# Attention's values on two column halves of the array, with normalised probabilities as the moving operand

## The reference

```python
s = jnp.einsum('bcqhgd,bcshd->bchgqs', qc, kb) * (A_HEAD_DIM ** -0.5)   # + bias, masked
m = jnp.maximum(jnp.max(s, axis=-1, keepdims=True), sink)
p = jnp.exp(s - m)
denom = jnp.sum(p, axis=-1, keepdims=True) + jnp.exp(sink - m)
o = jnp.einsum('bchgqs,bcshd->bcqhgd', p / denom, vb)
...
mix = jnp.concatenate([y_a, y_b], axis=-1)      # attention | retention
x = x + mix @ w_out
```

## Time and profile before

| | |
|---|---|
| median of 3 runs | 576.05 us (575.78 to 576.2) |
| the profiled execution's own time | 576.34 us |
| its span | 574.2 us |
| PE busy in the span | 549.9 us (96%) |
| DVE busy | 423.5 us (74%) |
| ACT busy | 359.3 us (63%) |
| mean granted TensorE clock | 0.995 |

### The profile page before, as it was taken

One profiled execution on the slowest core, in us unless ns is written; L12 is line 12 of the kernel. 1 busy time (PEld: TensorE's weight loads), 2 busy tenths in 40 slices (PEclk: granted clock), 3 DMA queues, 4 the chain that ended last, 5 costly groups with the idle time before them and its releaser, 6 DMA issues.

```text
span 574.2 us, 8097 instructions
## 1 busy us (share of the span) xinstructions
PE 549.9 (96%) x2782; PEld 451.3 (79%) x2783; DVE 423.5 (74%) x572; ACT 359.3 (63%) x477; POOL 116.7 (20%) x102
## 2 busy tenths in 40 slices
PE   3999999999999999998999999999999999999992
PEld 3988878888878888876788888888888888888860
DVE  2664577454764843377988889888898888988887
ACT  4563554781134363335778887788877888778823
POOL 3350000000000000002443234432244323411100
PEclk9999999999999999999999999999999999999998
DMA  8989212203020236677999999999999999999173
GB/s 299 373 277 387 58 36 74 74 20 128 1 73 1 74 111 226 231 276 272 344 390 373 371 366 365 368 367 335 346 372 389 372 359 374 369 389 339 34 294 146
DMA packets 72044, 144.32 MB, mean 251 GB/s; under 512 B 3794, under 2 KB 13322, under 8 KB 71888
## 3 DMA queue, kind: packets, MB, share of 16 engines
q1 hardware_dynamic: 65936, 124.96, 61.7%
q0 software_dynamic: 6080, 19.00, 9.5%
HBM read 132.77 MB, written 14.69 MB: 257 GB/s over the span
## 4 chain that ended last, share of the span: by engine, by line
PE 85%; DVE 6%; DMA 4%; issue 2%; ACT 1%; SPq 0%; POOL 0%; POOLq 0%; DVEq 0%
PE ps L1317 24%; PE ps L1319 23%; PE ps L1318 23%; PE ps L1324 6%; PE ps L1429 2%; PE ps L1466 2%; PE ps L1454 2%; DMA arena<-y_dram 1%; PE ps L1497 1%; PE ps L1399 1%; DMA arena<-norm_g 1%; PE ps L1420 1%; DVE res L1304 1%; DMA arena<-h_dram,meta 1%; PE ps L1337 1%
## 5 line engine op out<-in xcount | busy, mean ns | idle before, releaser
L1117 DVE TENSOR_TENSOR lo_ring<-arena,hi_ring 128x2048 fp32r<-128x2048 f32 x94 | 215.1, 2291 | 28.5 <-ACT hi_ring L808 27.4
L1317 PE MATMUL ps<-hi_ring,act_hi 128*128 128x512 f32 x576 | 232.6, 404 | 0.5 <-DVE act_lo L911 0.5
L1319 PE MATMUL ps<-hi_ring,act_lo 128*128 128x512 f32 x576 | 225.2, 391 | 0.0
L1318 PE MATMUL ps<-lo_ring,act_hi 128*128 128x512 f32 x576 | 224.7, 390 | 0.0
L808 ACT ACTIVATE hi_ring<-arena 128x2048 fp32r<-128x2048 f32 x94 | 180.2, 1917 | 18.6 <-PE ps L1319 18.6
L1317 PEld LDWEIGHTS ps<-hi_ring,act_hi 128*128 128x128 f32 x576 | 108.3, 188 | 27.4 <-issue 6.0
L1319 PEld LDWEIGHTS ps<-hi_ring,act_lo 128*128 128x128 f32 x576 | 108.1, 188 | 23.6
L1318 PEld LDWEIGHTS ps<-lo_ring,act_hi 128*128 128x128 f32 x576 | 108.4, 188 | 20.2
L901 DVE SCALAR_TENSOR_TENSOR lo_ring<-arena,over,hi_ring 128x512 fp32r<-128x512 f32 x40 | 29.4, 748 | 33.5 <-ACT hi_ring L640 33.5
L911 DVE TENSOR_TENSOR act_lo<-ps,act_hi 128x512 fp32r<-128x512 f32 x64 | 41.7, 683 | 11.6 <-ACT act_hi L669 5.8
L563 POOL DMA_INDIRECT y_dram<-y,row_info x15 | 16.1, 1073 | 149.6 <-issue 149.6
(11 more groups left out here) (197 smaller groups left out, 564.1 us busy)
## 6 DMA issues: line engine op xcount, KB each, us to landing
arena<-w_gate SPq DMA_DIRECT2D x32, 1024.0 KB, 15.2
arena<-w_up SPq DMA_DIRECT2D x32, 1024.0 KB, 15.8
arena<-w_down SPq DMA_DIRECT2D x32, 1024.0 KB, 15.6
arena<-w_in SPq DMA_DIRECT2D x16, 512.0 KB, 7.8
y_dram<-arena POOLq DMA_DIRECT2D x8, 512.0 KB, 11.8
arena<-w_out SPq DMA_DIRECT2D x4, 1024.0 KB, 5.2
arena<-y_dram SPq DMA_DIRECT2D x8, 512.0 KB, 7.1
arena<-w_in SPq DMA_DIRECT2D x3, 1024.0 KB, 12.9
```

Source lines behind the costliest of these rows:

```text
L1117: nc.vector.tensor_tensor(lo(N1 + n12), raw(n12), hi(N1 + n12).bitcast(F32), ALU.subtract).then_inc(lo_done, 1)
L1317: nc.tensor.matmul(dst, a_hi, b_hi, start=start, stop=False)
L1318: nc.tensor.matmul(dst, a_hi, b_lo, start=False, stop=False)
L1319: return nc.tensor.matmul(dst, a_lo, b_hi, start=False, stop=stop)
```

## The change

1. `softmax_denom` goes on: after the reciprocal, DVE multiplies the probabilities in `prob` (4 heads by 128 keys for u < 2, by 192 after that) by it and raises `p_scaled`. `turn_prob` waits for that where it waited for `exp_done`, and for the copies of the unit before.
2. `turn_prob` lays the four heads' transposes side by side, one bank per key block; ACT copies whole banks, into a buffer per key group.
3. `values` runs once per token tile instead of once per unit, in slots 5, 9, 13 and 17. The stationary operand is 64 columns of values, the moving one 512 columns of probabilities (4 heads by 128 queries), key group 0 writes PSUM partitions 0 to 63 and group 1 writes 64 to 127. The result is channels by tokens already; DVE copies it to `mix` (512 columns, four times) where it scaled 256 columns eight times.
4. `turn_mix(0)` goes. `mix_hi(0)` and `mix_lo(0)` read `mix` in SBUF, in slot 28. PE waits for the gate's silu (`silu_done`) in front of each tile of group 11 in its place.
5. The rows of `w_out` that belong to attention arrive in the new order of channels, in two transfers of 64 partitions in place of one of 128 (groups 11 and 13).

```diff
@@ DVE
                 step_done(nc.vector.reciprocal(r_denom, denom))
-
-            def attention_out(u):
-                t, kv = u // 2, u % 2
-                dve.wait_ge(o_ready, u + 1)
...
-                nc.vector.tensor_tensor(mix[:, t, 256 * kv:256 * kv + 256].rearrange("p (h c) -> p h c", h=4),
-                                        ps[:, 6, 0:256].rearrange("p (h c) -> p h c", h=4),
-                                        r_denom.unsqueeze(2).to_broadcast([P, 4, A_DIM]), ALU.mult).then_inc(mix_a, 1)
+                w0 = P if u < 2 else CHUNK
+                nc.vector.tensor_tensor(prob[:, :, w0:], prob[:, :, w0:],
+                                        r_denom.unsqueeze(2).to_broadcast([P, 4, 2 * P - w0]), ALU.mult).then_inc(p_scaled, 1)
+
+            def attention_out(t):
+                dve.wait_ge(o_ready, t + 1)
...
+                nc.vector.tensor_copy(mix[:, t, 0:512], ps[:, 6, :]).then_inc(mix_a, 1)
...
-                if k in VALUE_SLOTS:
-                    attention_out(VALUE_SLOTS.index(k))
+                if k in VALUE_SLOTS[1::2]:
+                    attention_out(VALUE_SLOTS.index(k) // 2)
@@ PE
             def turn_prob(u):
                 if u:
-                    pe.wait_ge(mix_a, u)
-                else:
-                    pe.wait_ge(va_copied, 1)
+                    pe.wait_ge(pt_copied, probs_value(u - 1))
+                if u >= 2:
+                    pe.wait_ge(mix_a, u // 2)
...
-                pe.wait_ge(exp_done, 4 * (u + 1))
...
+                pe.wait_ge(p_scaled, u + 1)
+                for b in range(1 if u < 2 else 0, 2):
+                    ins = turn(6 + b, [prob[:, hh, b * P:(b + 1) * P] for hh in range(4)])
                 ins.then_inc(p_turned, 1)
 
-            def values(u):
...
-                        ins = nc.tensor.matmul(ps[:, 6, hh * A_DIM:(hh + 1) * A_DIM], prob_t[:, hh, b, :],
-                                               va[:, t - 1 + b, kv * A_DIM:(kv + 1) * A_DIM], start=(b == b0), stop=(b == 1))
+            def values(t):
...
+                for b in range(b0, 2):
+                    for kv in range(2):
+                        rows = slice(kv * A_DIM, (kv + 1) * A_DIM)
+                        ins = nc.tensor.matmul(ps[rows, 6, :], va[:, t - 1 + b, rows], prob_t[kv][b],
+                                               start=(b == b0), stop=(b == 1))
                 ins.then_inc(o_ready, 1)
...
+                        pe.wait_ge(silu_done, T + t + 1)
...
-                if k == MIX_A_SLOT:
-                    turn_mix(0)
@@ SP
-                    sp.wait_ge(m_turned, 2 * T)
+                    sp.wait_ge(m_turned, T)
+                    sp.wait_ge(m_lo, T)
...
+                    if half == 0:
+                        for kv in range(2):
+                            sp.dma_start(as_chunks(dst)[kv * A_DIM:(kv + 1) * A_DIM, :, :],
+                                         w_out_heads[:, 4 * kv:4 * kv + 4, 512 * cols:512 * cols + 512]
+                                         ).then_inc(w1_in[slot1(g)], 16)
```

More of the change, by code:

```diff
@@ L94 @@
 SCM_OFF = (0, 512, 896, 1152)
+TWO_PART_OUT = (NA + NB, NA + NB + 2)
 def log_gamma(h):
@@ L118, in w1_value, with probs_value @@
 def w1_value(g):
-    return 16 * sum(2 if NA <= h < NA + NB else 1 for h in range(g % RING1, g + 1, RING1))
+    return 16 * sum(2 if NA <= h < NA + NB or h in TWO_PART_OUT else 1 for h in range(g % RING1, g + 1, RING1))
+def probs_value(u):
+    return u + 1 if u < 2 else 2 * u
 def build(nc, x, norm1_g, w_in, attn_sinks, rel_bias, ret_gn_g, w_out, norm2_g, rg_w, rg_b, re_w, re_b,
@@ L193, in build @@
         bias_pairs = region(O_BIAS, A_HEADS * WIN).rearrange("p (i a j) -> p a i j", i=4, a=2)
-        prob_t = region(O_PT, 1024).rearrange("p (h b q) -> p h b q", h=4, b=2)
+        prob_t = [[region(O_PT, 512), region(O_PT + 512, 512)],
+                  [region(O_MIX + b * D + 512, 512) for b in range(2)]]
         scm = region(O_SCM, 1280)
@@ L248, in build @@
         w_out_v = w_out.rearrange("a (k p) n -> p (a k) n", p=P)
+        w_out_heads = w_out.rearrange("a (k p) n -> p (a k) n", p=A_DIM)
         w_gate_v = w_gate.rearrange("a e (k p) n -> (a e) p k n", p=P)
@@ L700, in copy_prob_t @@
                 act.wait_ge(p_turned, u + 1)
[L701 to L704, removed]
+                for b in range(1 if u < 2 else 0, 2):
+                    nc.scalar.copy(prob_t[u % 2][b], ps[:, 6 + b, :]).then_inc(pt_copied, 1)
             def copy_rot(n):
@@ L711, in mix_hi @@
             def mix_hi(part):
+                if part == 0:
+                    act.wait_ge(mm_done, tile_value(NA + NB - 2, T - 1))
                 for t in range(T):
-                    act.wait_ge(m_turned, T * part + t + 1)
+                    if part:
+                        act.wait_ge(m_turned, t + 1)
+                        rows = ps[:, 4 + t, :]
+                    else:
+                        act.wait_ge(mix_a, t + 1)
+                        rows = mix[:, t, 0:512]
                     nc.scalar.activation(ht_hi[:, 4 * part:4 * part + 4, t * P:(t + 1) * P],
-                                         ps[:, 4 * part + t, :].rearrange("p (k s) -> p k s", k=4),
-                                         ACT.Copy).then_inc(m_hi, 1)
+                                         rows.rearrange("p (k s) -> p k s", k=4), ACT.Copy).then_inc(m_hi, 1)
             def copy_x2(half, t):
@@ L1049, in mix_lo @@
                 for t in range(T):
-                    row_lo(ht_lo[:, 4 * part:4 * part + 4, t * P:(t + 1) * P], 4 * part + t,
-                           ht_hi[:, 4 * part:4 * part + 4, t * P:(t + 1) * P], m_hi, T * part + t + 1, m_lo)
+                    rows = ps[:, 4 + t, :] if part else mix[:, t, 0:512]
+                    dve.wait_ge(m_hi, T * part + t + 1)
+                    nc.vector.tensor_tensor(ht_lo[:, 4 * part:4 * part + 4, t * P:(t + 1) * P],
+                                            rows.rearrange("p (k s) -> p k s", k=4),
+                                            ht_hi[:, 4 * part:4 * part + 4, t * P:(t + 1) * P].bitcast(F32),
+                                            ALU.subtract).then_inc(m_lo, 1)
             def norm2(t):
@@ L1468, in retention_values, with turn_mix @@
                 ins.then_inc(ro_ready, 1)
[L1470 to L1474, removed]
+            def turn_mix():
+                pe.wait_ge(mix_b, B_HEADS)
                 for t in range(T):
[L1476 to L1479, removed]
+                    turn(4 + t, [mix[:, t, 512 + i * P:512 + (i + 1) * P] for i in range(4)]).then_inc(m_turned, 1)
             def turn_x2(n):
@@ L1547, in _ @@
                     turn_v()
-                if k in VALUE_SLOTS:
-                    values(VALUE_SLOTS.index(k))
+                if k in VALUE_SLOTS[1::2]:
+                    values(VALUE_SLOTS.index(k) // 2)
                 if k in TURN_SLOTS:
@@ L1562, in _ @@
                 if k == MIX_B_SLOT:
-                    turn_mix(1)
+                    turn_mix()
                 if (g, t) in TURN_X2_STEPS:
```

25 lines of the change are left out of this document (11 added, 14 removed).

## The result

The changed kernel takes 599.58 us (598.7 to 601.09) against 576.12 us; the recorded ratio is 1.0368 with a 95% interval of 1.033 to 1.0405 (the quotient of these two medians alone is 1.041, just above it). The forecast was 592.0 us in a range of 588 to 597. The sign and the place were right, the size was too small by about a third: + 23.5 us by the medians (+ 21 by the ratio) against + 15.9.

The account below looks back on a forecast made before the run. PE was taken as the bound: + 16.7 (transposes later), + 0.4 (last values), - 1.7 (`turn_mix(0)` gone), + 0.5 (copy wait) = + 15.9 us on 576.34, 592.2; less 0.3 to the median, forecast 592.0, range 588 to 597.

Parts of the forecast that it names:

- What bounds the kernel: Attention and experts: PE is busy nearly throughout (71.97 of 73.00 us, 276.69 of 277.00), so added work or waits lengthen the time.
- The loop: Attention: each unit's transposes now wait for DVE's multiplication, closing a ring; seven turns sum to 79.47 us, last transposes 16.7 later.
- The 0.05 from DVE to PE: Attention: the step from the end of DVE's multiplication to PE's transposes, added to the multiplication's 0.95 us for 1.00.
- What PE saves is not on the path: Attention: PE's 7.8 us of work without values, against a ring of 12.0, leaves it idle; only slot 17's values count.
- the rival of the wait never felt: Attention: DVE's product is ready before PE wants it, so only PE's savings stay, - 5.6 us, 570.5; chance 0.04.
- The values on halves: Attention: four 512-column matmuls, two passes each, run in pairs; 2.1 us at slot 17 against 1.7 before, + 0.4.
- the wait of 0.5 for the last copy of values: Retention, slot 31: its values now stand right behind the tile and need ACT's last copy of the values; + 0.5 us.
- The clock: Rival, attention: the clock falls in PE's new gaps of about 4.2 us, costing 2 to 7 us, 594 to 599; chance 0.18.
- its own sign of being wrong: Changed profile: waits at the transposes below 1 us, clock below full inside the mixers, or PE idle less in the experts.
- The other side: Rival, attention: with 2.7 us of slack on DVE the wait is never felt and the time is 570.5; chance 0.04.
- not idle by choice: Attention: DVE's split at 85.14 waits for ACT's split, exponentials, logits and PE's scores in turn, so DVE has no slack.

Follow-up runs that it names:

- e8_fill_keep: The changed kernel with idle matmuls in front of the eight transposes and eight more in front of the first expert's rows; 591.89 us, ratio 1.0231.
- e2_early: The changed kernel with DVE's denominator, reciprocal and multiplication moved from slot 2u+2 to slot 2u, in front of that slot's split; 573.33 us, ratio 0.9916.
- e3_loop_only: The kernel before with only DVE's multiplication added, PE's transposes waiting for it and the output copied unscaled, no column halves; 602.37 us, ratio 1.0425.
- e1_fill: The changed kernel with 5 to 17 idle identity multiplications on PE in front of each unit's wait for the scaled probabilities; 596.05 us, ratio 1.0323.
- e11_after_split: e2_early with DVE's scaling one instruction later, behind the split of slot 2u instead of in front of it; 580.69 us, ratio 1.0053.

## Why the prediction was wrong

- *What bounds the kernel* was right: PE has no slack, and DVE's place in the queue is read from the timelines, not from busy shares. e8_fill_keep and e2_early show both.
- *The loop*, + 16.7 us of starts shifted: right. Without falls of the clock (e8_fill_keep) every loop lies within 0.05 us of its sum, and the whole distance is + 16.4 against the sum's + 15.9. Even with the falls five of seven loops lie within 0.35 us. e3_loop_only shows the loop as the cause by itself. The 0.05 from DVE to PE had no row of before behind it; it measures 0.05 in e8_fill_keep and up to 0.15 in the changed kernel.
- *What PE saves is not on the path*: right in the changed kernel. e2_early brings the savings out once the loop is short: 3.9 us, less than the 5.6 that the rival of the wait never felt had summed, and with 1.4 us of waits for the multiplication left.
- *The values on halves*: taken as 2.1 us a call, measured 1.87. The pass of 0.46 us was read from a row of 2.32 that contains the last matmul's run through the array; by the starts a pass is 0.43. `turn_mix(0)` and the wait of 0.5 for the last copy of values came about as priced: behind the last transposes e8_fill_keep is 0.6 us shorter than before, against 0.4 - 1.7 + 0.5 = - 0.8.
- *The clock*: this is the step that failed. I set it aside as a rival with a chance of 0.18, at 594 to 599, on the argument that the clock fell 3.6 us after PE's last matmul before, so that only the two gaps of some 4.2 us could reach it, and put it at nothing in the sum. That was a threshold from one case. The clock fell during or behind waits of 1.79, 2.62, 2.73, 2.29 and 4.44 us, and did not behind 1.51 and 2.50; five falls where I had two at most. They cost 5.6 us in the distance (e1_fill and e8_fill_keep against the changed kernel). Loop by loop against e8_fill_keep, the falls at 64.1 and 84.6 cost 0.1 and 0.3 us, since PE would have waited there anyway; those at 94.9 and 132.4 cost 1.8 and 1.6, since they slow the transposes and scores, which are on the loop; and the one at 146.1 costs 1.6 behind the last transposes, where PE's own work is the bound again. So the price of 1.8 a fall was about right and the count was not. With the sixth fall before the first expert, + 1.6, and 16.4 less 0.3, that is the span's 23.3. The condition was mis-sized, and with it the chance. A clock below full inside the mixers was also what the prediction named as its own sign of being wrong.
- *The other side*, a wait never felt, was wrong for this order and would be right for another: to have the product on DVE at least 2.7 us earlier is what e2_early does. What I called not idle by choice was, in one place: DVE stood idle in front of its split, with the exponentials due before the split's own input.

## What to carry to other kernels

When a change puts an engine's result in front of another's next step, add up the whole ring from step to step, the unrelated instructions queued between included, and compare it with the bound engine's own work per turn. If the ring is longer, first look for an idle time of the producer at which the inputs are there already: a split and three small instructions that changed places were worth 8 us here (e11_after_split against e2_early). And if a bound TensorE gets waits like these, seven of 1.5 to 4.4 us within 90 us, put falls of its clock into the sum, each at what it takes from work on the ring or behind it: they came with five of these seven, and in every profiled kernel here that had such waits.

## What the runs showed of the hardware

- The clock fell during or behind idle times of 1.79 to 4.44 us, and once (64.1) nearly 2 us after PE had taken up work again at 62.3. Another idle time of 2.50 us had no fall. The gap before the first expert was followed by one after 2.45, 2.25 and 2.18 us (changed, e1_fill, e2_early) and not after 2.33 (before). The length of one gap alone does not decide. At the lower level neighbouring matmuls of a tile start 0.43 us apart and not 0.23.
- Idle matmuls in the gaps kept the clock up in all of the mixers and were worth 5.6 us, though PE did more.
- The passes of float32 matmuls on column halves run two at a time (four matmuls of 512 columns, eight passes, in 1.87 us, against 0.43 for a single pass), and the program's order of the halves within a call did not matter.
